# A two-block fp32 transformer kernel: loads, residuals and splits in another order at layer 1's feed-forward entry, the keys' norm as exp(-ln/2), and cross-attention scores ahead of the last query tile

## What is computed

```python
for l in range(DEPTH):                       # DEPTH = 2
    x = x + 0.5 * swiglu_ffn(rms_norm(x, ffn1_norm_g[l]), ffn1_w_in[l], ffn1_w_out[l])
    proj = rms_norm(x, mix_norm_g[l]) @ w_mix_in[l]
    ...                                      # y_rwkv, y_moba
    x = x + concatenate([y_rwkv, y_moba]) @ w_mix_out[l]
    x = x + memory_cross_attention(rms_norm(x, xattn_norm_g[l]), rms_norm(mem, mem_norm_g[l]), ...)
    x = x + 0.5 * swiglu_ffn(rms_norm(x, ffn2_norm_g[l]), ffn2_w_in[l], ffn2_w_out[l])

# in rwkv7_time_mix, the keys' norm, per head of 64:
kk = kk / jnp.maximum(jnp.sqrt(jnp.sum(kk * kk, axis=-1, keepdims=True)), 1e-12)

# memory_cross_attention: 4 heads of 256, no mask
q = (h @ w_q).reshape(B, S, 4, 256)
logits = einsum('bshd,bmhd->bhsm', q, k) * 256 ** -0.5
o = einsum('bhsm,bmhd->bshd', softmax(logits), v) @ w_o
```

## Time and profile before

| | |
|---|---|
| median of 3 runs | 2735.25 us (2735.14 to 2738.49) |
| the profiled execution | 2739.51 us, of which the span of instructions is 2737.5 us |
| PE busy | 2635.0 us, 96% |
| PE weight load busy | 2326.4 us, 85% |
| DVE / ACT / POOL busy | 1700.8 / 1027.9 / 99.2 us |
| mean granted clock of PE | 0.972 of 2.4 GHz |
| DMA | 415.63 MB, mean 152 GB/s |

### The profile page before, as it was taken

The page is one execution under the profiler, slowest core; times in us unless marked ns, Lnnn a source line. Parts: engine busy times, 40 slices in busy tenths (PEclk is TensorE's granted clock), DMA queues, the critical chain, the costliest instruction groups (busy, mean ns, idle before and its releaser), DMA issues. The chain is left out here.

```text
span 2737.5 us, 44684 instructions
## 1 busy us (share of the span) xinstructions
PE 2635.0 (96%) x18787; PEld 2326.4 (85%) x18787; DVE 1700.8 (62%) x2283; ACT 1027.9 (38%) x1275; POOL 99.2 (4%) x179
## 2 busy tenths in 40 slices
PE   8999989999999999989999999999999999989999
PEld 7999888989999999779899944355799899737999
DVE  6887655768868877656688732553455555354555
ACT  4335302444334354114443321643333333264333
POOL 2110000001101100000001000000000000000000
PEclk9999988999999999989999999879999999999999
DMA  8775301647766774004457751100455555210452
GB/s 277 261 260 185 93 1 36 204 147 242 264 217 230 261 234 145 14 1 147 162 193 261 245 202 62 46 1 31 130 184 182 197 185 185 78 62 31 140 183 93
DMA packets 279510, 415.63 MB, mean 152 GB/s; under 512 B 10105, under 2 KB 235721, under 8 KB 277698
## 3 DMA queue, kind: packets, MB, share of 16 engines
q1 hardware_dynamic: 260332, 348.16, 38.4%
q0 software_dynamic: 18128, 64.20, 6.7%
q10 hardware_dynamic: 902, 1.15, 0.2%
HBM read 399.82 MB, written 13.65 MB: 151 GB/s over the span
## 5 line engine op out<-in xcount | busy, mean ns | idle before, releaser
L619 PE MATMUL ps<-h_high,w_low 128*128 128x256 f32 x2016 | 571.0, 283 | 0.0
L617 PE MATMUL ps<-h_high,w_high 128*128 128x256 f32 x1952 | 557.5, 286 | 12.3 <-DVE h_low L1399 5.9
L617 PEld LDWEIGHTS ps<-h_high,w_high 128*128 128x128 f32 x1952 | 375.2, 192 | 15.0 <-issue 5.5
L619 PEld LDWEIGHTS ps<-h_high,w_low 128*128 128x128 f32 x2016 | 387.5, 192 | 0.0
L1414 DVE TENSOR_TENSOR w_low<-ring,w_high 128x2048 fp32r<-128x2048 f32 x131 | 300.0, 2290 | 138.3 <-ACT w_high L1155 138.0
L618 PE MATMUL ps<-h_low,w_high 128*128 128x256 f32 x1312 | 371.9, 283 | 0.0
L2805 DVE TENSOR_TENSOR w_low<-ring,w_high 128x2048 fp32r<-128x2048 f32 x96 | 220.0, 2292 | 240.9 <-ACT w_high L2589 240.7
L1155 ACT ACTIVATE w_high<-ring 128x2048 fp32r<-128x2048 f32 x131 | 250.3, 1915 | 269.5 <-DMA ring<-in_ffn_w_in 152.3
L2589 ACT ACTIVATE w_high<-ring 128x2048 fp32r<-128x2048 f32 x96 | 183.8, 1916 | 331.5 <-PE ps L2268 304.2
L618 PEld LDWEIGHTS ps<-h_low,w_high 128*128 128x128 f32 x1312 | 252.6, 193 | 0.0
L1435 DVE SCALAR_TENSOR_TENSOR mod_acc<-wmod,cond,mod_acc 128x512 f32<-128x512 f32 x336 | 230.8, 748 | 0.0
(11 more groups left out here) (432 smaller groups left out, 5435.2 us busy)
## 6 DMA issues: line engine op xcount, KB each, us to landing
ring<-in_w_mlp SPq DMA_DIRECT2D x96, 1024.0 KB, 5.5
ring<-in_ffn_w_in SPq DMA_DIRECT2D x88, 1024.0 KB, 8.9
wmod<-in_w_mod POOLq DMA_DIRECT2D x96, 512.0 KB, 6.3
ring<-in_ffn_w_out SPq DMA_DIRECT2D x44, 1024.0 KB, 5.1
ring<-in_w_mix_in SPq DMA_DIRECT2D x26, 1024.0 KB, 5.5
ring<-in_xattn_w_kv SPq DMA_DIRECT2D x16, 1024.0 KB, 5.3
mod_scratch<-mod_acc POOLq DMA_DIRECT2D x24, 512.0 KB, 5.4
ring<-mod_scratch SPq DMA_DIRECT2D x12, 1024.0 KB, 6.7
```

Source lines behind the costliest of these rows:

```text
L617: mm(dst, w_hi, x_hi, start=start, stop=False, **more)
L619: return mm(dst, w_lo, x_hi, start=False, stop=stop, **more)
```

## The change

At layer 1's first feed-forward SP issues the first six loads as gate 0, up 0, gate 1, up 1, down 1, down 0, and its loop starts with the next pair of steps. ACT and DVE split only gate 0 before the residuals, then up 0 and gate 1 behind them in `norm`; up 1 is split on ACT right after `norm` and on DVE right after `first_scaled`. PE runs the whole gate first, then the whole up.

The keys' norm becomes `max` of the sums with 1e-24 on DVE straight out of PSUM, `Ln` and `Exp(-x/2)` on ACT, and the product on DVE. The table set that holds both is loaded once, before the exponentials of n = 5, and the load in the key/value tiles is gone.

In cross-attention the scores of heads 0 to 2 stand before query tile 3 on PE, each behind its own `xq_evac`; head 2 uses bank 5 and head 3 bank 4. `softmax` is cut into parts that ACT and DVE call in a new order, and query tile 3 and output tile 1 use `w_high[5]`. One piece of `modulate` is cut in two and output tile 1's split moves behind the first outputs.

```diff
-COLUMN_HIGHS = (... + [0, 2, 0, 2] + [0, 3, 2, 3]
+COLUMN_HIGHS = (... + [0, 2, 0, 2] + [0, 3, 2, 5]
+CROSS_BANKS = (0, 1, 5, 4)
@@ SP, ffn
-            with sp.Fori(1 if f == 0 and l == 0 else 0, FFN_STEPS // 2) as j:
+            if f == 0 and l:
+                for r, b in ((0, 0), (1, 0), (0, 1), (1, 1), (2, 1), (2, 0)):
+                    tile(b, r, b, 0)
+            with sp.Fori(1 if f == 0 else 0, FFN_STEPS // 2) as j:
@@ PE, first_gate_up
+                else:
+                    for r in range(2):
+                        hi, lo = parts(r, 0, r, first_buffers(l, f)[r])
+                        for p in range(KD // 2):
+                            if r == 0:
+                                for q in ((), (1, 2), (3,), ())[p]:
+                                    sums(l, 0, q)
+                                gained_pair(l, 0, p)
+                            first_part(r, p, hi, lo)
@@ PE, cross
             def scores(h):
+                pe.wait_ge(*xq_evac.at(l, h + 1))
-            pe.wait_ge(*xq_evac.at(l, LIN_TILES))
-            for h in range(XH + 3):
...
@@ PE, main
             for j in range(LIN_TILES):
                 column_tile(l, ("xq", j), xq_bank(j), h_high, late_low, before=None if j else xq_pair)
-            cross(l)
+                if j == LIN_TILES - 2:
+                    for h in range(3):
+                        cross_scores(h)
+            cross_turn(0)
+            cross_turn(1)
+            cross_scores(3)
+            cross_av(0)
+            cross_turn(2)
+            cross_av(1)
+            cross_turn(3)
+            cross_av(2)
+            cross_av(3)
@@ ACT, first_high
-            for r in range(2):
-                w_high_part(FfnTiles(l, f), r, 0, 0, first_buffers(l, f)[r])
+            w_high_part(FfnTiles(l, f), 0, 0, 0, first_buffers(l, f)[0])
@@ ACT, norm, behind the squares
+            if n == 0 and l:
+                w_high_part(FfnTiles(l, 0), 1, 0, 0, first_buffers(l, 0)[1])
@@ ACT, behind norm(l, 0)
+            if l:
+                w_high_part(FfnTiles(l, 0), 1, 1, 0, 0, (0, 0, 0))
@@ ACT, mixer
+                    nc.scalar.preload_act_table_set(LN_EXP)
                     act.wait_ge(*dve_step.at(l, DVE_CUM))
...
-                    act.wait_ge(*hs_done.at(l, 1))
-                    for i in range(2):
-                        go(sgt[:, 2 * i:2 * i + 2, :], ps[2 + i]..., ACT.Sqrt).then_inc(*act_step.up())
+                    act.wait_ge(*dve_step.at(l, DVE_KK_SS))
+                    go(sgt[:, :, :], sgt[:, :, :], ACT.Ln).then_inc(*act_step.up())
+                    act.wait_ge(*act_step.now(l))
+                    go(sgt[:, :, :], sgt[:, :, :], ACT.Exp, scale=-0.5).then_inc(*act_step.up())
...
-                    nc.scalar.preload_act_table_set(LN_EXP)
@@ ACT, cross-attention
-            col_high(l, XQ0 + 3, XQ0 + 1)
+            col_high(l, XQ0 + 3)
             col_high(l, XO0)
-            col_high(l, XO0 + 1)
-            softmax(l, XH, NH, XD ** -0.5, (T, T), cross_part)
+            exponential, turned = softmax(l, NH, XD ** -0.5, (T, T), CROSS_BANKS)
+            for h in range(3):
+                exponential(h)
+            turned(0)
+            turned(1)
+            exponential(3)
+            for h in range(XH):
+                cross_part(l, h)
+                if h < 2:
+                    turned(h + 2)
+                if h == 0:
+                    col_high(l, XO0 + 1, XQ0 + 3)
@@ DVE, norm
+            if n == 0 and l:
+                first_low(l, 0, (1,))
@@ DVE, ffn, behind first_scaled
+                if not f:
+                    w_low_of(1, 1, 3, 0)
@@ DVE, ffn, before the residual
-                first_low(l + 1, 0)
+                first_low(l + 1, 0, (0,))
@@ DVE, mixer
             col_low(l, 9)
+            dve.wait_ge(*hs_done.at(l, 1))
+            step(l, v.tensor_scalar(sgt[...], psum[:, 2:4, :], 1e-24, None, ALU.max))
             col_low(l, 10)
             dve.wait_ge(*act_step.at(l, ACT_KK_STD))
-            step(l, v.tensor_scalar(sgt[:, :, :], sgt[:, :, :], 1e-12, None, ALU.max))
-            step(l, v.reciprocal(sgt[:, :, :], sgt[:, :, :]))
             step(l, v.tensor_tensor(kk_t, kk_t, sgt[:, :, :], ALU.mult))
             col_low(l, 11)
@@ DVE, cross-attention
             xq_scaled(l, 2)
-            modulate(l, 0, second, range(4, 6))
-            col_low(l, XO0 + 1)
+            modulate(l, 0, second, range(4, 5))
+            maxima, weights = softmax(l, NH, XD ** -0.5, (T, T), CROSS_BANKS)
+            evac = cross_out(l)
+            for h in range(3):
+                maxima(h)
+            modulate(l, 0, second, range(5, 6))
+            for h in range(3):
+                weights(h)
             xq_scaled(l, 3)
-            softmax(l, XH, NH, XD ** -0.5, (T, T), cross_out(l))
+            maxima(3)
+            weights(3)
+            for h in range(XH):
+                evac(h)
+                if h == 1:
+                    col_low(l, XO0 + 1)
```

175 lines of the change are left out of this document (92 added, 83 removed).

## The result

| | before | after |
|---|---|---|
| median | 2735.19 us (2715.96 to 2738.49, 4 runs) | 2695.51 us (2686.02 to 2703.17, 4 runs) |
| ratio, 95% interval | | 0.9863 (0.9837 to 0.9889) |
| span of the profiled execution | 2737.5 us | 2690.7 us |
| mean granted clock of PE in it | 0.972 | 0.979 |
| PE idle in it (span less busy) | 102.5 us | 80.2 us |

The account below looks back on a forecast made before the run. PE was taken to bound the kernel, busy 2635.0 of 2737.5 us. Idle 26.1 plus clock 3.1, 29.2 us, off the median 2735.25 gave 2706.1 with both clock falls, 2709.1 without; forecast 2708.0, range 2700 to 2718.

Parts of the forecast that it names:

- Part A: Entry of layer 1's feed-forward: five PE stalls gone, 8.4 us of idle with tails, plus 1.4 us of clock.
- the thinnest (rest of down 0): Layer 1's first down product: rest of down 0 ready at 821.6, wanted at 822.9, a cover of 1.3 us.
- Part B: Keys' norm, both layers: PE stalls at tiles 11 and 12 nearly gone, 6.4 us idle, plus 1.7 us clock.
- tails: About 0.16 us added to each PE bracket, because a stopping matmul's tail is drawn as work.
- The table load's stall: Key/value tiles: PE's 1.15 us idle before the first token-major tile gone or nearly, 2.5 us for both layers.
- Part C: Cross-attention, both layers: PE's waits mostly covered, 4.9 - 0.5 = 4.4 us a layer, 8.8 us together.
- The idle terms together: PE idle time removed across the change's places: 8.4 + 6.4 + 2.5 + 8.8 = 26.1 us.
- The clock term: Half clock behind two layer 1 stalls, feed-forward entry (1.4) and keys' norm (1.7), goes away: 3.1 us together.
- 1, a cover fails: Splits at down 0, tile 11 or tile 12 come late, 2.3 to 2.7 us a place: 2715 us; chance 0.17.
- 2, the clock: Half-clock stretch from 1760.4 to 1811.6 ends later, 2714 us, chance 0.13; or the other way, 2701, chance 0.05.
- 3, tables not held: The attention's Exp loads its own table set again, the 2.5 us are lost: 2710.5 us; chance 0.04.
- 4, slower than before: Half-clock stretch grows or one falls among the feed-forward's matmuls: 2736 to 2742 us; chance 0.02.

Follow-up runs that it names:

- e11: Kernel after with SP's loads at layer 1's entry in the old order: 2692.41 us, one execution.
- e12: Kernel after with gate and up alternating again in layer 1's first products: 2705.80 us, one execution.
- e7: Kernel after with the activation table load kept in the key/value tiles: 2692.96 us, ratio 0.9868 to the kernel before.
- e1: Kernel after run once more without edit, beside the kernel before: 2691.22 us, ratio 0.9845.
- e8: Kernel after with 14 useless matmuls per layer in PE's waits at the second block's attentions: 2684.16 us, ratio 0.9823 to the kernel before.
- e9: Kernel before with the same 14 useless matmuls per layer at the same places as e8: 2712.25 us, ratio 0.9916 to the kernel before.
- e6: Kernel after with eight useless matmuls some 120 us ahead of the second block's first attention: 2706.26 us, ratio 0.9896 to the kernel before.
- d4: Kernel after with four useless matmuls (1.73 us) shortly ahead of the second block's first attention: 2686.85 us, ratio 0.9815 to the kernel before.
- d1: Kernel before with four useless matmuls (1.73 us) some 30 us ahead of the second block's first attention: 2733.04 us, ratio 0.9982.
- d2: Kernel before with two useless matmuls (0.87 us) at the same place as d1: 2719.68 us, ratio 0.9942.
- e10: e8 with more useless matmuls in the waits of the first block's recurrence: 2683.80 us, ratio 0.9814 to the kernel before.

## Why the prediction was wrong, by its steps

**Part A held.** The five stalls are gone. The load order took the three around the second gate tile (e11), the place of the splits the other two, and gate before up was needed for it (e12). No cover failed, the thinnest (rest of down 0) included. Three can be read: up 0's rest 1.7 us (2 forecast), the last 1.8 (rest of up 1 ready at 802.3, wanted at 792.6 + 2 x 5.76 = 804.1; 1.9 forecast), and gate 1's normalised part 3.0 (3). Alone it measured 9.2 at full clock, a reading that leaves the clock's share out, against 8.4 of idle in the sum.

**Part B held.** The max took 1.22 us (1.23 taken), the logarithm and the exponential 1.06 each (1.2 estimated). The rest of tile 11 waits for the rounding, as forecast, and neither that tile nor tile 12 has a bracket: the 0.1 left for tile 12 wasn't there. The sum took tile 12's 0.35 us for both layers; the trace of the kernel before has it in layer 0 alone (302.34, layer 1 has none), so the idle there was 6.1 with tails and not 6.6. The table load's stall is gone in both layers, and e7 brings it back with its 1.15 us.

**Part C held.** One bracket of 0.19 us a layer is left, where 0.1 and 0.4 were set aside. It stands at the last head's output, as forecast, and ACT's rounding of output tile 1 is behind it, as forecast, but by another way: that rounding (to 563.96) holds up head 1's rounded output, DVE's rest of it is there at 565.24, and only then is the bank free; `probT` of the last head is there at 564.93. The forecast counted five tails a layer where there are four brackets (1.43, 0.74, 0.74 and 1.17). With its tail the one left costs 0.35 of the 0.5 set aside.

**The idle terms together:** 26.1 forecast. The places of the change have 18 brackets with 23.7 us in the trace of the kernel before and two with 0.4 in that after: 23.3 us, and with 16 tails of 0.16 us 25.9. That is the reading that doesn't hang on the clock. At full clock e1 has 25.9 as well, the three parts 28.4, and e8 against e9 29.4.

**The clock term failed.** The sum had 3.1 us for two falls. The step that failed is the argument that the clock's pattern moves little because four executions lie within 4.4 us. The scatter of a kernel tells what the pattern does while the kernel stays as it is. A change that moves stalls by microseconds picks another pattern, and this one picked a shorter one. Between e1 and its reference 43.1 us were gained, and between e8 and e9, in which the attention's half clock is gone on both sides, 28.1. So 15.0 us of the gain, give or take some 5, go away when the waits ahead of the second block's attentions are filled on both sides, in stages that the change doesn't touch. The two profiles of the stage account for 9.6 of it (127.7 less 118.1). What is left I put down to executions with shorter stretches, such as the profiled ones of e6 and e7; of the timed executions only the mean clock is known (up to 0.983 for the kernel after), so that last share is argued, not shown. The fill on the kernel after, worth 7.1 us where the two profiled attentions differ by 14.8, points the same way.

**The first block also gained a little more** than the terms. In six profiles with the first block of before, the second block begins at 1575.8 to 1583.8, mean 1581.0; in five with that of after (after, e1, e6, e8, d4) at 1544.6 to 1551.5, mean 1549.0. That is 32 against 29.2. The pair in the first profiles has 38.1, because two falls of 6.8 us, some 35 us ahead of the first product with `state` (at 343.9 and 1129.0 in the kernel before), are missing in that execution of after, about 3 us each; e1 has both. A single pair of profiles would have misled by 6 us.

**The rivals.** 1, a cover fails: none did. 2, the clock: its place was right ("it may as well go the other way: 2701"), its price and its chance were not. The good side was what happened, and I gave it 0.05. It also reached further than 2701: half of the 51.2 us of the earlier trace rows is 25.6, which from 2708.0 gives 2682. 3, tables not held: there is no second load. 4, slower than before: no run. Its own argument shows the asymmetry that I should have used. The kernel before sat in nearly the worst pattern that any profile shows, 58.0 us of 61.4, and by the times left it in three of 62 executions. From there a change of pattern could mostly gain. So the side was to be seen from the rows; that this change brought a shorter pattern, and how much shorter, was luck as far as the runs show.

**What the sum needed:** the forecast at equal clock, 2735.25 - 29.2, and beside it the stage's half clock, anything from nothing gained to 25.6 us. A range from 2682 up to the forecast would have come out of rows that I had.

**What stays open.** Which of the rows an execution takes hangs on shifts of 1 to 2 us close to the stage (d1, d2, d4) and on something in its earlier course (four of ten in d1). What that is stays open, and so does why d4's clock stays up over the same waits. Why the kernel after lands mostly in the shorter ones isn't shown; that its own edits raise the clock there isn't needed, since kernels with the whole change have 37.5, 3.4 and 0 us, and with the fills both versions have the same clock. The 2.5 us between the parts and the whole stays open too; it is within what the reading at full clock can be wrong by.

## What to carry to other kernels

Where a profile has a long stretch at half clock with PE busy, look at the idle time just ahead of it, and price a change twice: at equal clock, and for that stretch lengthened or gone. Compare two versions with their clock falls removed on both sides (a few useless matmuls in PE's waits) or over many executions; single profiles mislead by what the clock did. Such a fill can be worth as much as the edits: 14 matmuls a layer gave 22 us before the change and 7 after it. A delay is no safe substitute: four matmuls helped in four executions of ten on one kernel (d1), and eight made the kernel after 15 us slower (e6).

## What the runs showed of the hardware

The clock can be at 1.2 GHz for 30 to 55 us while PE is drawn as busy in all of it (30.70 of 30.70, 51.20 of 51.20), and the same matmuls ran at 2.4 GHz throughout where PE's waits just before were filled (e8: 102.66 of 103.30 busy, clock 1.00). In the kernel before, the waits that precede it are short; timeline of PE, its first two:

```profile
1748.98 0.67 PE L2446 MATMUL ps<-km,consts_sb 96*96 96x256 f32 x2 [0.99 <-DVE km L2914]
1751.12 1.17 PE L2446 MATMUL ps<-km,consts_sb 96*96 96x256 f32 x2 [1.47 <-DVE km L2914]
1752.08 4.68 PE L2450 MATMUL ps<-ring,cc 128*128 128x384 f32 x7
```

Two waits of 0.99 and 1.47 us and one of 1.62 behind the first scores are followed by a loss of up to 24 us. They needn't be: the same three waits are in d4, and nothing is lost. The Trainium skill, "TensorE: Matmul & The Clock Gate", section "Part 1: The HAM clock gate", says of the slow matmuls at a kernel's start that their number varies from run to run and that the penalty is under 1% of a typical span. The start agrees: the first stretch at half clock is 3.4 us long in the kernel before and 6.8 in the kernel after, so at most 3.4 us are lost. Over the whole kernel it is more: 154.4 us at half clock in the profile before, up to 77 us by an estimate at half their length, 2.8% of the span, of which 24 lie in this one stage. Where a change is worth 1%, that is more than what is to be measured.

What half clock costs differs by stage. In the attention it is nearly the full half: 2.81 us a unit at half clock, 1.43 at full, and 0.45 of the half-clock time over the stage. In the recurrence it is 0.2 to 0.3 (17 profiles, 68.4 to 71.7 us in layer 1). Fills there took most of what they gave: 68.6 us at a granted clock of 0.88 and 68.2 at 0.98 (stretch rows of e8 and e10).
